# A norm as a factor per token, the first head's queries in halves, and four early weight tiles

## The reference

```python
x = x + cat @ w_out[l]
x = x + peer_ffn(rmsnorm(x, norm_ffn[l]), ...)

def peer_ffn(xn, wq, subkeys, u_tab, v_tab):       # 8 heads, 16 experts a head
    q = (xn @ wq)                                  # per head two halves of 128
    sc = einsum(q, subkeys)                        # 2 x 128 scores per token and head
    top_s, top_i = top_k(sc, 16)
    best, ci = top_k(sums of pairs of top_s, 16)   # 16 experts of 16384
    g = softmax(best)
    act = gelu(u_tab[idx] . xn)
    return sum(g * act * v_tab[idx])
```

## Time and profile before

| | |
|---|---|
| median of 3 runs | 2244.35 us (2235.81 to 2244.74) |
| the profiled execution | 2239.58 us, of which the span is 2237.8 us |
| TensorE, VectorE, ScalarE, GpSimd busy | 83%, 61%, 37%, 31% |
| moved by DMA | 660.9 MB, 536.9 of it in gathers |
| mean of TensorE's granted clock | 0.929 |

### The profile page before, as it was taken

How to read it: one execution, slowest core, us unless ns; L and a number is a source line. 1 busy time by engine, 2 the same in 40 slices (tenths; PEclk the granted TensorE clock), 3 DMA queues, 4 the chain that set the end, 5 groups by cost and what they waited for, 6 DMA issues and landing times. The chain is left out here.

```text
span 2237.8 us, 22571 instructions
## 1 busy us (share of the span) xinstructions
PE 1858.2 (83%) x7332; PEld 1163.2 (52%) x7332; DVE 1362.2 (61%) x3102; ACT 833.9 (37%) x2287; POOL 684.2 (31%) x586
## 2 busy tenths in 40 slices
PE   7988797788787788799879788788777776899797
PEld 6957543343332232696664343343222255799796
DVE  7657767567657645665766647756755555374732
ACT  4340334344343333434124433434334355264231
POOL 4000254444454342400015444444444300000320
PEclk9978899999999999996989999999999998898998
DMA  5426899999999999442679999999999942353001
GB/s 201 130 78 263 319 419 422 421 421 421 421 421 421 422 421 387 162 149 78 263 275 401 421 420 421 421 422 421 421 421 421 421 154 93 113 171 104 1 1 47
DMA packets 107685, 660.90 MB, mean 295 GB/s; under 512 B 11952, under 2 KB 13360, under 8 KB 41648
## 3 DMA queue, kind: packets, MB, share of 16 engines
q0 software_dynamic: 73728, 536.90, 57.8%
q1 hardware_dynamic: 33840, 122.56, 15.5%
HBM read 658.37 MB, written 1.05 MB: 295 GB/s over the span
## 5 line engine op out<-in xcount | busy, mean ns | idle before, releaser
L566 PE MATMUL banks<-big 128*128 128x512 f32 x1680 | 810.8, 625 | 208.7 <-ACT big L753 207.7
L820 POOL DMA_INDIRECT big<-in_experts,big x420 | 474.3, 1129 | 935.1 <-PE banks L566 564.5
L1073 DVE SCALAR_TENSOR_TENSOR big<-big 128x1024 bf16<-128x1024 f32 x420 | 509.6, 1226 | 402.5 <-DMA big<-in_experts,big 402.0
L566 PEld LDWEIGHTS banks<-big 128*128 128x128 f32 x1680 | 313.9, 197 | 687.6 <-ACT big L753 372.5
L745 ACT ACTIVATE big<-big 128x1 f32<-128x1 f32 x512 | 102.0, 199 | 558.5 <-DVE big L1073 552.2
L753 ACT ACTIVATE big<-constants,big 128x128 f32<-128x128 f32 x512 | 205.6, 402 | 59.6 <-PE banks L566 12.9
L566 PE MATMUL banks<-expert_rows,big 128*128 128x512 f32 x368 | 174.5, 608 | 28.5 <-ACT big L753 28.4
L1073 DVE SCALAR_TENSOR_TENSOR big<-expert_rows,big 128x1024 bf16<-128x1024 f32 x92 | 112.0, 1225 | 81.0 <-DMA expert_rows<-in_experts,big 80.9
L749 ACT ACTIVATE big<-big 128x1 f32<-128x1 f32 x512 | 150.8, 294 | 17.6
L1377 PE MATMUL banks<-x_parts,chunk_parts 128*128 128x256 f32 x1104 | 140.0, 290 | 6.3 <-DVE chunk_parts L1367 6.3
L1377 PEld LDWEIGHTS banks<-x_parts,chunk_parts 128*128 128x128 f32 x1104 | 137.9, 197 | 7.5 <-issue 5.2
(11 more groups left out here) (349 smaller groups left out, 2138.0 us busy)
## 6 DMA issues: line engine op xcount, KB each, us to landing
big<-in_ada SPq DMA_DIRECT2D x48, 512.0 KB, 7.6
weight_ring<-in_w_in SPq DMA_DIRECT2D x40, 512.0 KB, 4.6
weight_ring<-in_wq SPq DMA_DIRECT2D x32, 512.0 KB, 8.2
weight_ring<-in_gdn_in SPq DMA_DIRECT2D x32, 512.0 KB, 3.4
weight_ring<-in_w_out SPq DMA_DIRECT2D x16, 640.0 KB, 5.3
weight_ring<-in_lru_in SPq DMA_DIRECT2D x16, 512.0 KB, 4.5
big<-in_experts,big POOLq DMA_INDIRECT x420
weight_ring<-in_w_kv SPq DMA_DIRECT2D x8, 512.0 KB, 3.7
```

The costliest lines, as they stand in the source:

```text
L566: last = nc.tensor.matmul(sums_e[tt][:, c * 512:(c + 1) * 512], diag[:, v % NDIAG], rows_e[v % NBUF][:, D + c * 512:D + (c + 1) * 512], st ...
L820: nc.gpsimd.indirect_dma_start(rows_e[v % NBUF], None, d_e, bass.IndirectOffsetOnAxis(ap=expert[:, h, tt, a:a + 1], axis=0)).then_inc(arri ...
L1073: nc.vector.scalar_tensor_tensor(waste[:, v % 2], rows_e[v % NBUF][:, 0:D], 1.0, x_rows[:, tt], ALU.mult, ALU.mult, accum_out=dots[:, v:v ...
```

## The change

It has three parts, in both layers.

The norm ahead of the experts becomes a factor per token. VectorE multiplies each tile of `xT` by the gain alone, right in the loop of the out projection, so `xn` no longer holds the factor 1/rms. `token_sums` adds up the squares with the squares as the stationary operand and one column of ones, so that the sums lie with tokens on the partitions, two columns in all (`rstd_e` after root and reciprocal). The factor is applied where tokens are on the partitions: in the copies of the scores, now two per head (`score_part`), and in the copy of `x_rows`.

Head 0's two query tiles are computed by token half (`first_query(m, tt)`), in the order (0, 0), sums, (1, 0), (0, 1), scores of half 0, (1, 1), scores of half 1. The first choice waits for half 0 alone (`score_early`).

The weights of query tiles 4 to 7 (heads 2 and 3) no longer go through the ring. SyncE loads them at ring tile 4 of the layer into the last two row buffers. GpSimd's gathers 9 and 10 then wait for their use (`ahead_used`).

```diff
+WQ_AHEAD = (4, 5, 6, 7)
+N_RING = N_WQ + 2 * PH - len(WQ_AHEAD)
...
+    def first_query_bank(m, tt):
+        return nc_ps[m if tt else 4 + m][:, 0:P]
+    def score_bank(h, tt):
+        bank = 6 if h == 0 and tt == 0 else 2 + h % 2
+        return nc_ps[bank][:, 2 * tt * P:2 * (tt + 1) * P]
+    ahead_at = {m: (NBUF - 2 + i // 2, i % 2) for i, m in enumerate(WQ_AHEAD)}
...
@@ sync
+                    if n == WSLOTS:
+                        for m in WQ_AHEAD:
+                            sp.dma_start(query_weights(m), d_wq[l, m]).then_inc(s("ahead_loaded"), 16)
@@ tensor
+                def token_sums(k):
+                    pe.wait_ge(s("sq_ffn"), k + 1)
+                    for tt in range(NT):
+                        last = nc.tensor.matmul(nc_ps[2 + tt][:, 511:512], sq[:, k, tt * P:(tt + 1) * P], ones[:, 0:1],
+                                                start=(k == 0), stop=(k == KD - 1))
+                    return last
...
                     if m >= 1:
-                        total(nc_ps[0][:, 0:T], sq, "sq_ffn", m - 1, 1, m == 1, False)
-                total(nc_ps[0][:, 0:T], sq, "sq_ffn", KD - 1, 1, False, True).then_inc(s("sum_ffn"), 1)
+                        token_sums(m - 1)
...
+                def first_query(m, tt):
+                    wt = w_tile(N_WQ + m)[:, 0:D].rearrange("p (k c) -> p k c", k=KD)
+                    for k in range(KD):
+                        if m == 0 and tt == 0:
+                            pe.wait_ge(s("ffn_ready"), k + 1)
+                        last = nc.tensor.matmul(first_query_bank(m, tt), wt[:, k], xn[:, k, tt * P:(tt + 1) * P],
+                                                start=(k == 0), stop=(k == KD - 1))
+                    return last
...
+                def first_scores(tt):
+                    for j in range(2):
+                        last = nc.tensor.matmul(score_bank(0, tt)[:, j * P:(j + 1) * P], query[:, j, tt * P:(tt + 1) * P],
+                                                sub[:, j], start=True, stop=True)
+                    return last
...
-                query_tile(0)
-                query_tile(1)
+                first_query(0, 0)
+                token_sums(KD - 1).then_inc(s("sum_ffn"), 1)
+                first_query(1, 0).then_inc(s("query_half"), 1)
+                first_query(0, 1).then_inc(s("w_used"), 1)
                 pe.wait_ge(s("sub_loaded"), 32)
-                key_scores(0)
+                pe.wait_ge(s("query_half_kept"), 1)
+                first_scores(0).then_inc(s("score_half"), 1)
+                first_query(1, 1).then_inc(s("w_used"), 1)
+                pe.wait_ge(s("query_kept"), 2)
+                pe.wait_ge(s("root_ffn"), 1)
+                first_scores(1).then_inc(s("score_ready"), 1)
                 pe.wait_ge(s("out_added"), KD)
+                pe.wait_ge(s("score_early"), 1)
                 turn_x(0)
@@ scalar
-                root(nc_ps[0][:, 0:T], rms[:, 0], T, D, "sum_ffn", "root_ffn")
+                for tt in range(NT):
+                    last = nc.scalar.activation(rstd_e[:, tt:tt + 1], nc_ps[2 + tt][:, 511:512], ACT.Sqrt, scale=1.0 / D, bias=eps)
...
+                def score_part(h, tt):
+                    return nc.scalar.activation(score[:, h % 4, 2 * tt:2 * tt + 2],
+                                                score_bank(h, tt).rearrange("p (a c) -> p a c", a=2),
+                                                ACT.Copy, scale=rstd_e[:, tt:tt + 1])
...
-                    nc.scalar.copy(score[:, h % 4], nc_ps[2 + h % 2][:, :].rearrange("p (a c) -> p a c", a=2 * NT)).then_inc(s("score_kept"), 1)
+                    if h > 0:
+                        score_part(h, 0)
+                    score_part(h, 1).then_inc(s("score_kept"), 1)
...
+                act.wait_ge(s("query_half"), 1)
+                for m in range(2):
+                    last = nc.scalar.copy(query[:, m, 0:P], first_query_bank(m, 0))
+                last.then_inc(s("query_half_kept"), 1)
+                act.wait_ge(s("score_half"), 1)
+                act.wait_ge(s("rstd_ffn"), 1)
+                score_part(0, 0).then_inc(s("score_early"), 1)
@@ gpsimd
+                    if v in (NBUF - 2, NBUF - 1):
+                        pool.wait_ge(s("ahead_used"), 2 * (v - NBUF + 3))
@@ vector, in the loop of the out projection, behind the modulation tiles
-                recip(rms[:, 0], "root_ffn", "rstd_ffn")
-                normed(xn, xT, par[:, C_NFFN:C_NFFN + KD], rms[:, 0], "rstd_ffn", "ffn_ready")
+                    dve.wait_ge(s("out_added"), m + 1)
+                    nc.vector.tensor_scalar(xn[:, m], xT[:, m], par[:, C_NFFN + m:C_NFFN + m + 1], None, ALU.mult).then_inc(s("ffn_ready"), 1)
+                recip(rstd_e, "root_ffn", "rstd_ffn")
...
-                        dve.wait_ge(s("score_kept"), ha + 1)
+                        if ha == 0 and at_a[0] == 0:
+                            dve.wait_ge(s("score_early"), 1)
+                        else:
+                            dve.wait_ge(s("score_kept"), ha + 1)
```

More of the change, by code:

```diff
@@ L212, in first_block @@
     r.at = C_GROUP
+    rstd_e = r(8)[:, 0:NT]
     query = r(4, T)
@@ L256, in first_block, with query_weights, query_at @@
         arrived(f"rows_loaded{i}")
+    ahead_at = {m: (NBUF - 2 + i // 2, i % 2) for i, m in enumerate(WQ_AHEAD)}
+    def query_weights(m):
+        if m in ahead_at:
+            buffer, half = ahead_at[m]
+            return rows_e[buffer][:, half * D:(half + 1) * D]
+        return wring[:, query_at(m) % WSLOTS, 0:D]
+    def query_at(m):
+        return N_WQ + m - sum(a < m for a in WQ_AHEAD)
     def unit(v):
```

32 lines of the change are left out of this document (23 added, 9 removed).

## The result

The kernel after took 2216.26 us, median of 4 runs (2210.55 to 2220.79), beside 2243.1 us for the kernel before in the same rounds: ratio 0.9889, 95% interval 0.9864 to 0.9914. The profiled execution took 2220.79 us (span 2219.0), 18.8 less than the one of before.

What follows compares the result with a forecast made beforehand. The expert stage was taken as bound by full DMA engines from gather 11. (8.5 - 1.1) + 7.1 = 14.5 us off the profiled 2239.6 gave 2225.1, plus 4.8 to the median 2229.9, called 2230; range 2220 to 2241.

Steps and rivals of the forecast that it cites:

- A: In times such as A+5.95: the end of the last addition to `xT` in a layer, from which times are counted.
- rival C: Head 0's half tiles cost as much as whole ones, by unhidden weight loads: gain 0 to 1 us, 2244; chance 0.04.
- Rival A: TensorE's low clock comes anyway behind the last addition, losing 2.85 us a layer: gain about 9, 2235; chance 0.15.
- What they give: Early loads: 2 MB fewer beside the first gathers, all ahead of gather 11 where DMA engines run dry: worth 0.
- The bound of 5 us a layer: Upper bound on the early loads' worth in the expert stage, were that stage full from gather 0.
- The chain's own term: Shorter chain to gather 11: 8.5 us less 1.1 for refill in layer 0, 7.1 in layer 1; 14.5 in all.
- the true start of the full stage: Expert stage: the full DMA stretch was taken to start at gather 11, not gather 0, so gather 11's move counts.
- Rival B: All of the earlier start is kept, the expert stage being full from gather 0: gain 24 us, 2220; chance 0.06.
- One sign of the forecast: Expert stage from gather 11 to the last row: a length change of more than 2 us would make the prediction wrong.
- the 10 that were to make the prediction wrong: Gather 11 moving by less than 5 or more than 10 us would make the prediction wrong.
- Rival D: VectorE's waits without releaser grow, 2 us each on the chain to `down(0)`; up to 2257; slower 0.05, same 0.1.
- Rival E: The early loads delay the first stage, ahead of the last addition, by 2.5 us a layer: 2235; chance 0.05.

Runs made afterwards that it cites:

- No early loads, same chip: Kernel after with all query tiles through the ring and gathers 9 and 10 unheld, on chip d beside after: 2225.4 us, ratio 0.9922 to before.
- before again: The kernel before, unchanged, profiled once more on chip b; one run, no median or ratio given.

## Why the prediction was wrong

**Right, by its own steps.** The first choice at A+5.95 (forecast 6.4, of which 0.4 stood for the seventh multiplication, which ends ahead of A), gather 0 at A+14.7 (15.1), VectorE's new wait of 1.64 us (1.6), head 1's choice at A+19.5 (20.0), TensorE at 2.4 GHz through the chain in layer 0, gather 10 23.2 us after gather 0 (27), and in layer 0 a deeper DMA dip (289 GB/s from 264 to 268, against 322 in the earlier trace rows; in layer 1 it is 293 where it was 285). Two half tiles took 3.82 us where 3.58 were taken, so rival C is out; by this row too consecutive 128-column matmuls with loads of their own are 0.119 us apart. That is against the rule of the Trainium skill (TensorE: Matmul & The Clock Gate, section The mechanism) that a load overlaps matmuls only when row groups differ; the same section also lets a load run ahead when it goes to the background weight buffer, and which of the two these loads did no run here shows. Rival A happens, but rarely: in 3 of 22 profiled layers with half tiles gather 0 was 1.6 to 2.9 us late (17.6, 17.0 and 16.3), each time with a granted clock of 0.50, the 1.2 GHz level, for 3 to 7 us around A. "No early loads, same chip", layer 1, two windows of 2 us, one in that spell and one behind it:

```profile
1112.00:1114.00 2.00, 1.92 (x8) 1.71 (x8) 0.71 (x3) 0.42 (x1) 0.00 (x0) 0.50 0.02 6
...
1120.00:1122.00 2.00, 1.88 (x17) 1.69 (x16) 1.33 (x9) 0.71 (x3) 0.00 (x0) 1.00 0.65 168
```

**The step that failed** is "What they give: ... all of it ahead of gather 11, where the DMA engines run dry anyway: 0". In before they did not run dry there at all, and in after hardly; the dry windows of the earlier trace rows lie behind gather 11. The 6 us ahead of it in layer 0, before and after:

```profile
265.31:271.31 6.00, 4.03 (x5) 1.85 (x6) 1.49 (x3) 4.68 (x16) 0.00 (x1) 0.61 1.02 420
```

```profile
257.00:263.00 6.00, 4.02 (x5) 1.83 (x6) 4.63 (x18) 4.69 (x16) 0.00 (x0) 0.59 0.95 397
```

So most of the 2 MB a layer had not been in a dry spell: with the chain and gather 11 unchanged (chip a), all that was gone was gone from behind gather 11, two thirds of it from behind A+80, and the loads took 4.0 and 3.9 us off the two layers. On chip d it was 3.4 and 5.5 (up to 2.3 of it the clock's spell), and by another way: there the engines did run dry just ahead of gather 11, and gather 11 itself came 3.2 and 5.4 us sooner, with VectorE's shorter waits. The bound of 5 us a layer that stood beside the 0 was nearly the value; the sum should have read 14.5 + 8 for what lies behind A. The chain's own term, 14.5, was small too: 15.3 on chip d, 21.0 on chip a and, with whole tiles, 16.8 on chip b. Its move of gather 11, forecast as 8.5 and 7.1, is 7.4 and 7.8 on chip d and 10.6 and 10.5 on chip a, where VectorE has no waits.

**Its reason** was the sentence that the true start of the full stage is gather 11 and not gather 0. It is neither by itself. Holding gather 11 by 5.5 us cost 4.8 on the mean, which speaks for it; holding gather 0 by 15.6 with gather 11 sooner cost 9.0, which speaks against it. Rival B, "the stage being full from gather 0", had the right size (2220) for half of the right reason. One sign of the forecast came out for it: gather 11 to the last gather was to change by no more than 2 us, and it went from 604.7 to 603.6 and from 604.2 to 604.9. On chip d it holds as well (602.8 and 604.0, then 602.2 and 604.2). That is luck: in both profiles of before, VectorE's waits, which the forecast did not count as holding gather 11, had kept it back until 14.8 to 15.6 MB were moved. From "before again", without such waits, 607.7 and 607.6, it would have changed by 4.1 and 2.7.

**The rest.** Gather 11 moved by 12.8 and 15.2 us, beyond the 10 that were to make the prediction wrong; some 5 us of each is VectorE's waits, which the first profile had and the second had not. On one chip it is 10.6 and 13.2. Rival D, that these waits grow, is out: on chip d they are 1.7 us in layer 0, where they were 4.8. Rival E is not settled. The profiles say that the early loads are worth 8 to 9 us behind A. The medians say 2 by themselves (0.9991, whose interval reaches to 5.6 us), 1 on chip d, where the ratios say nothing (0.9925 beside 0.9922), and 9 on chip a for the kernel that moved the exponentials as well (0.9891 beside 0.9933). Part of the difference may be lost ahead of A, where the unsure 3 us of layer 1 are; but on chip d the two stretches ahead of A add up to 458.1 us in both profiles, and there it is most likely which executions were profiled, the slowest of one kernel and the fastest of the other. How much of the 8 us reaches the kernel's time is open, and with it how much of the 10 us by which the forecast missed.

**How large the gain is.** The ratio of after was 0.9889 first and 0.9925 (0.9907 to 0.9942) on another chip; together 17 to 25 us. The forecast's 0.65% lies inside the second interval and outside the first. The two intervals barely meet, and kernels that differ from after only by moved loads or exponentials, by idle waits or by whole tiles for head 0 lay at 0.9864 to 0.9913 on chips a, b and c. So the spread from chip to chip is wider than one interval tells.

## What to carry to other kernels

Where a stage is bound by one full resource, don't look for the event at which it starts. Add up what the resource has moved by a fixed time at which it is full in both kernels, and what is left to move; the end follows from the two numbers, and a date counts only for the bytes that it adds or withholds. Bytes taken out of such a stage count even where the edit that took them moves no date.

Before reading a difference between two profiles as the change's, profile the old kernel again: here 5 us of waits on each layer's chain came with the chip, and the first stage ahead of A was 211.9, 214.4 and 217.3 us in three executions of the kernel before and 216.4, 213.0 and 217.2 in three of after. A profile is also one execution out of several: see whether it was a slow or a quick one of its kernel.

## What the runs showed that I had not expected

- VectorE waits of 0.2 to 3.3 us between dependent instructions, 1.7 to 5 us in all in one choice and decoding, on three chips (and in the first profile of before) and never on two others, only with gathers issued beside it. What they wait for stays open.
- The transfer rate of the expert stage is 420.8 to 421.2 GB/s in each of 40 profiled layers, on each chip, worked out as bytes over time from A+80 to the last gather.
- The stage ahead of A differs by 4 us between two executions of one kernel (213.0 and 217.2 for after), as much as the early loads bring in a layer.
- A wait that is already met costs VectorE about 0.05 us (64 took 3.1 us), which is not nothing at the head of a chain.
